# Shift and scale of a modulation: summed on VectorE along rows instead of collected on TensorE in one-column products

## The reference

```python
def adaln_pre_norm(x, c, g, w_mod, b_mod):
    mod = jax.nn.silu(c) @ w_mod + b_mod
    shift, scale, gate = jnp.split(mod, 3, axis=-1)
    h = rms_norm_2(x, g, NORM_EPS) * (1.0 + scale[:, None, :]) + shift[:, None, :]
    return h, gate
...
for i in range(DEPTH):
    h, gate = adaln_pre_norm(x, c, norm_g[i], w_mod[i], b_mod[i])
    ...
    x = x + gate[:, None, :] * y
```

## Time and profile before

| what | value |
|---|---|
| runs, median of 3 | 1061.03 us |
| the profiled execution's own time, given by its span from first to last instruction | 1066.7 us |
| TensorE busy | 1048.1 us (98%) |
| VectorE busy | 771.7 us (72%) |
| ScalarE busy | 590.3 us (55%) |
| POOL busy | 120.4 us (11%) |
| chain that ended last | TensorE 88%, VectorE 6% |

### The profile page before, as it was taken

One profiled execution on the slowest core, in us unless ns is written; L12 is line 12 of the kernel. 1 busy time (PEld: TensorE's weight loads), 2 busy tenths in 40 slices (PEclk: granted clock), 3 DMA queues, 4 the chain that ended last, 5 costly groups with the idle time before them and its releaser, 6 DMA issues.

```text
span 1066.7 us, 25458 instructions
## 1 busy us (share of the span) xinstructions
PE 1048.1 (98%) x10480; PEld 996.2 (93%) x10485; DVE 771.7 (72%) x1090; ACT 590.3 (55%) x900; POOL 120.4 (11%) x131
## 2 busy tenths in 40 slices
PE   9999999999999999999999999999999999999997
PEld 8966999999999899997899999999998999999985
DVE  5987666766789689768766676786676877775586
ACT  6586555555456783334555454564544667666452
POOL 0230010100000028841000000000000000000000
PEclk9999999999999999999999999999999999999999
DMA  8734687888634510002678777737653656556401
GB/s 308 251 90 137 216 286 266 271 296 280 204 122 155 163 61 5 3 11 74 217 250 287 255 252 264 276 121 228 197 192 112 212 181 199 171 195 196 143 2 59
DMA packets 83073, 192.23 MB, mean 180 GB/s; under 512 B 6000, under 2 KB 6912, under 8 KB 82992
## 3 DMA queue, kind: packets, MB, share of 16 engines
q1 hardware_dynamic: 74256, 159.93, 45.3%
q0 software_dynamic: 7584, 27.53, 7.8%
q10 hardware_dynamic: 1152, 3.59, 1.0%
HBM read 189.45 MB, written 1.05 MB: 179 GB/s over the span
## 4 chain that ended last, share of the span: by engine, by line
PE 88%; DVE 6%; issue 2%; ACT 2%; DMA 2%; POOL 0%; DVEq 0%; POOLq 0%; ACTq 0%
PE bank L2308 13%; PE bank L2310 13%; PE bank L2309 13%; PE bank L2659 5%; PE bank L2658 5%; PE bank L2660 5%; PE bank L2325 4%; PE bank L2345 4%; PE bank L2877 4%; PE bank L2275 2%; PE bank L2276 2%; PE bank L2277 2%; PE bank L2263 1%; PE bank L2265 1%; PE bank L2264 1%
## 5 line engine op out<-in xcount | busy, mean ns | idle before, releaser
L1350 DVE TENSOR_TENSOR w_lo<-raw,w_hi 128x1024 fp32r<-128x1024 f32 x295 | 357.8, 1223 | 199.2 <-ACT w_hi L737 198.7
L737 ACT ACTIVATE w_hi<-raw 128x1024 fp32r<-128x1024 f32 x295 | 310.3, 1059 | 291.4 <-PE bank L2310 150.4
L2308 PE MATMUL bank<-act_hi,w_hi 128*128 128x256 f32 x1200 | 334.0, 278 | 0.4 <-DVE w_lo L1350 0.3
L2309 PE MATMUL bank<-act_lo,w_hi 128*128 128x256 f32 x1200 | 332.9, 277 | 0.0
L2310 PE MATMUL bank<-act_hi,w_lo 128*128 128x256 f32 x1200 | 332.8, 277 | 0.0
L2308 PEld LDWEIGHTS bank<-act_hi,w_hi 128*128 128x128 f32 x1200 | 225.3, 188 | 1.7 <-DVE w_lo L1350 0.9
L2310 PEld LDWEIGHTS bank<-act_hi,w_lo 128*128 128x128 f32 x1200 | 225.3, 188 | 0.0
L2309 PEld LDWEIGHTS bank<-act_lo,w_hi 128*128 128x128 f32 x1200 | 225.0, 187 | 0.0
L2658 PE MATMUL bank<-w_hi,ff_hi 128*128 128x256 f32 x512 | 141.5, 276 | 0.0
L2659 PE MATMUL bank<-w_lo,ff_hi 128*128 128x256 f32 x512 | 141.5, 276 | 0.0
L2660 PE MATMUL bank<-w_hi,ff_lo 128*128 128x256 f32 x512 | 141.5, 276 | 0.0
(11 more groups left out here) (375 smaller groups left out, 1675.4 us busy)
## 6 DMA issues: line engine op xcount, KB each, us to landing
raw<-in_mlp_w_up_dram SPq DMA_DIRECT2D x64, 512.0 KB, 3.7
raw<-in_mlp_w_down_dram SPq DMA_DIRECT2D x64, 512.0 KB, 6.1
raw<-in_dil_w_in_dram SPq DMA_DIRECT2D x64, 512.0 KB, 4.1
mod_w<-in_w_mod_dram POOLq DMA_DIRECT2D x48, 512.0 KB, 5.9
raw<-in_conv_w_in_dram SPq DMA_DIRECT2D x32, 512.0 KB, 4.5
raw<-in_rwkv_w_rkv_dram SPq DMA_DIRECT2D x24, 512.0 KB, 4.1
raw<-in_dsa_w_in_dram SPq DMA_DIRECT2D x12, 512.0 KB, 8.1
raw<-in_dsa_w_o_dram SPq DMA_DIRECT2D x8, 512.0 KB, 4.5
```

Of the source, the lines that this page charges most:

```text
L737: act.activation(w_hi[:, slot, :], raw[:, slot, :], ACT.Copy).then_inc(hi_ready, 1)
L1350: dve.tensor_tensor(w_lo[:, slot, :], raw[:, slot, :], w_hi[:, slot, :].bitcast(F32), ALU.subtract).then_inc(lo_ready, 1)
L2308: pe.matmul(dst, w_hi[:, slot, at], hi[:, kt, :], start=begin, stop=False, skip_group_check=True)
L2309: pe.matmul(dst, w_hi[:, slot, at], lo[:, kt, :], start=False, stop=False, skip_group_check=True)
```

## The change

For shift and scale, the host lays `w_mod` out transposed: step k of part n brings output features 128k to 128k+127 as partitions, with the 1024 inputs along the row. silu(c) is needed as a row on all partitions: POOL loads `c_2` broadcast into `cond_row` ahead of each layer's weights, and ScalarE applies Silu to it in the MLP's first step, between the rounding of granule 7 and the relu. `weigh_mod` for shift and scale is then one VectorE instruction per step, a product of the two tiles with the sum along the row written as one column of `mod_col`. It writes the product back over `mod_w`. The gate part stays as it was. `mod_columns` goes, with both TensorE waits for its results; VectorE's addition of the bias reads `mod_col` in SBUF instead of PSUM. The number of weight bytes is the same.

```diff
         def mlp_plan(t):
-                        mod_all=t("mod_all", [P, 3 * D]),
+                        cond_row=t("cond_row", [P, D]), mod_unused=t("mod_unused", [P, D]), mod_gate=t("mod_gate", [P, D]),
...
             def modulation(l, between=()):
-                w = A["w_mod_2"][l].rearrange("(k p) (n c) -> n k p c", p=P, c=D)
+                w = A["w_mod_2"][l]
...
+                if l:
+                    for n in range(2):
+                        pool.wait_ge(mod_used[n], done)
+                pool.dma_start(M["cond_row"][:, :], A["c_2"][0].partition_broadcast(P)).then_inc(mod_loaded[0], 16)
...
-                def step(it, first_bank):
+                def step(it, first_bank, layer=None):
                     if isinstance(it, int):
                         split_block(base, 4, it)
+                        act.wait_ge(mod_loaded[0], 16 * (KT * layer + 2 + layer))
+                        act.activation(M["cond_row"][:, :], M["cond_row"][:, :], ACT.Silu).then_inc(cond_ready, 1)
                         relu(it, first_bank)
...
             def weigh_mod(l, n, k):
-                part, total = M["mod_w"][:, n, :], M["mod_all"][:, n * D:(n + 1) * D]
...
+                part = M["mod_w"][:, n, :]
+                rows = 16 * (KT * l + 1) + (16 * (l + 1) if n == 0 else 0)
+                dve.wait_ge(mod_loaded[n], k * 16 + rows)
+                if n < 2:
+                    if isinstance(k, int) and k == 0:
+                        dve.wait_ge(cond_ready, l + 2)
+                    to = mod_col[:, l, KT * n + k:KT * n + k + 1] if isinstance(k, int) else mod_col[:, l, bass.ds(k + KT * n, 1)]
+                    dve.scalar_tensor_tensor(part, part, 1.0, M["cond_row"][:, :], ALU.mult, ALU.mult,
+                                             accum_out=to).then_inc(mod_used[n], 1)
+                    return
+                total = M["mod_gate"][:, :]
...
             def modulation(l):
-                dve.wait_ge(mod_full, 4 * l + 2)
-                dve.tensor_tensor(mod_col[:, l, :], bank[(1, 3)[l]][:, 0:2 * KT], B_MOD[l], ALU.add).then_inc(mod_ready, 1)
+                for n in range(2):
+                    dve.wait_ge(mod_used[n], KT * (l + 1))
+                dve.tensor_tensor(mod_col[:, l, :], mod_col[:, l, :], B_MOD[l], ALU.add).then_inc(mod_ready, 1)
...
-            def mod_columns(l, part):
-                if part == 0:
-                    for n in range(2 if l else 3):
-                        pe.wait_ge(mod_used[n], KT * (l + 1))
...
-                for k in range(KT * part, KT * (part + 1)):
-                    mm = pe.matmul(bank[(1, 3)[l]][:, k:k + 1], M["mod_all"][:, k * P:(k + 1) * P], ones[:, 0:1], start=True, stop=True)
-                mm.then_inc(mod_full, 1)
...
             def rwkv_in():
-                turn_scaled(1, X, RKV_TURN, lambda: mod_columns(0, 0))
-                mod_columns(0, 1)
+                turn_scaled(1, X, RKV_TURN)
+                pe.wait_ge(mod_used[2], KT)
+                pe.wait_ge(up_relu, 2 * FF_STEPS)
                 mod_gate(0, (4, 5))
                 mod_gate(1, (4, 5))
...
-                    if n == 0:
-                        pe.wait_ge(mod_ready, 1)
...
                 fill(2, 1)
-                mod_columns(1, 0)
                 turn_scaled(2, xn, LATE_TURN)
-                mod_columns(1, 1)
...
-                            if n == 1 and half == q == 0:
-                                pe.wait_ge(mod_ready, 5)
```

More of the change, by code:

```diff
@@ L989, in step @@
                         split_hi(base, 8 + q, it)
-                step(0, 6)
+                step(0, 6, l)
                 with act.Fori(1, FF_STEPS - 1) as it:
@@ L1654, in weigh_mod @@
             def weigh_mod(l, n, k):
-                part, total = M["mod_w"][:, n, :], M["mod_all"][:, n * D:(n + 1) * D]
-                if isinstance(k, int):
-                    dve.wait_ge(mod_loaded[n], 16 * (KT * l + k + 1))
-                else:
-                    dve.wait_ge(mod_loaded[n], k * 16 + 16 * (KT * l + 1))
+                part = M["mod_w"][:, n, :]
[9 more added lines that the diff above has]
+                total = M["mod_gate"][:, :]
                 if isinstance(k, int) and k == 0:
@@ L1759, in gate_rows @@
                 for n, b in enumerate(banks):
-                    dve.wait_ge(mod_full, 4 * l + 3 + n)
+                    dve.wait_ge(mod_full, 2 * l + 1 + n)
                     to = gate[:, l, n * BLOCK:(n + 1) * BLOCK]
@@ L2712, in fill @@
                     pe.matmul(bank[b][:, 0:SEQ], ones, const[:, 0:SEQ], start=True, stop=True)
-            def mod_columns(l, part):
-                if part == 0:
-                    for n in range(2 if l else 3):
-                        pe.wait_ge(mod_used[n], KT * (l + 1))
-                    if l:
-                        pe.wait_ge(x_updated, 15)
-                    else:
-                        pe.wait_ge(up_relu, 2 * FF_STEPS)
-                for k in range(KT * part, KT * (part + 1)):
-                    mm = pe.matmul(bank[(1, 3)[l]][:, k:k + 1], M["mod_all"][:, k * P:(k + 1) * P], ones[:, 0:1], start=True, stop=True)
-                mm.then_inc(mod_full, 1)
             def mod_gate(n, banks=(5, 3)):
-                at = 2 * D + n * BLOCK
-                pe.matmul(bank[banks[n]][:, :], ones, M["mod_all"][:, at:at + BLOCK], start=True, stop=True).then_inc(mod_full, 1)
+                at = n * BLOCK
+                pe.matmul(bank[banks[n]][:, :], ones, M["mod_gate"][:, at:at + BLOCK], start=True, stop=True).then_inc(mod_full, 1)
             def rwkv_in():
                 base = STREAM["rkv"]
-                turn_scaled(1, X, RKV_TURN, lambda: mod_columns(0, 0))
-                mod_columns(0, 1)
+                turn_scaled(1, X, RKV_TURN)
+                pe.wait_ge(mod_used[2], KT)
+                pe.wait_ge(up_relu, 2 * FF_STEPS)
                 mod_gate(0, (4, 5))
@@ L3218, in laid_out @@
     arrays["w_iq"] = np.ascontiguousarray(iq.transpose(1, 0, 2, 4, 3, 5)).reshape(P, KT, IQ_COLS)
+    turned = arrays["w_mod_2"][:, :, :2 * D].reshape(2, D, 2, KT, P).transpose(0, 2, 3, 4, 1)
+    plain = arrays["w_mod_2"][:, :, 2 * D:].reshape(2, 1, KT, P, D)
+    arrays["w_mod_2"] = np.ascontiguousarray(np.concatenate([turned, plain], 1))
     arrays["const"] = np.concatenate([v.reshape(P, -1) for v in parts.values()], 1)
```

## The result

The changed kernel takes 1069.57 us (median of 15 runs, 1064.47 to 1072.71), the kernel before in the same comparison 1061.72 us (15 runs, 1060.56 to 1068.31). The ratio is 1.0065, 95% interval [1.0049, 1.008]: slower, by 7.85 us between the medians, outside the forecast's range.

A forecast was written before the change was run, and what follows sets the result against it. TensorE was taken as the bound (busy 1048.1 of 1066.7 us), in close races with VectorE at both entries. Terms -1.04 - 0.31, with 0 for VectorE's sums and ScalarE, gave -1.35: from median 1061.03 to 1059.7 us, range 1057.3 to 1063.7.

The forecast's parts named there:

- Entry of rkv, -1.04: Start of rkv: without the one-column products the second tile's turn and xx come 1.04 us earlier, then TensorE waits for the diagonal.
- Entry of conv, -0.31: Start of conv: of two bunches, 3.36 us, only 0.31 us is gained at the second block, VectorE being late next.
- VectorE's sums, 0: Weighings in the MLPs: 32 of 48 become summing products, 0.15 us more each, hidden by idle time; term 0.
- d: Extra time per VectorE summing instruction over the plain form's 1278 ns; taken as 0.15 us, at most 1.44.
- the upper bound: VectorE's summing form costed like the scan: four times 680 ns is 2720, 1.44 us more than the plain 1278 ns.
- the third rival: MLP ends: summing form slow, additions to X late; 1064.5 us at the upper bound, near 1063.5 at half rate; chance 0.12.
- ScalarE, 0: First step of each MLP: table load and pass, 2.34 us ahead of the relu, fit within 4.57 us of cover; term 0.
- the fourth rival: TensorE's waits at the entries lower its clock to 1.2 GHz, entry granules take twice as long; near 1070 us; chance 0.05.
- Behind both entries TensorE sets the pace again, and the gain stays: After the starts of rkv and conv: the gains of 1.04 and 0.31 us last, with nothing lost later.
- The stretches concerned do not depend on it, so I take the same difference from the median: Whole kernel: the median lies 5.7 us below the profiled span; the same -1.35 us is applied to it, giving 1059.7.
- the first two terms: The gains at the entries of rkv and conv, -1.04 and -0.31 us.

## Why the prediction was wrong

The two profiles, followed through the same marks, start times in us:

| mark | before | after | gain (-) or loss between marks |
|---|---|---|---|
| diagonal at rkv's entry | 295.90 | 295.01 | -0.89, first stage, differs between executions |
| first w_lo of rkv | 300.39 | 298.63 | -0.87, where the forecast had -1.04 |
| first w_lo at conv's entry | 703.12 | 701.15 | -0.21: +0.14 in the scan, -0.35 behind it, neither forecast |
| conv, block 2 | 718.12 | 715.81 | -0.34, the forecast's -0.31 |
| dil, first product | 822.92 | 823.71 | +3.10, nearly all of it the slow pitch in conv |
| end of the span | 1066.7 | 1066.2 | -1.29, late dil fast again in after (-1.6) |
| outside the span | +1.7 | +2.4 | +0.7 |

Point by point:

- *Entry of rkv, -1.04*: the mechanism was right, and the size near: 0.87. The second turn did start 1.03 earlier net of the lead, but `xx` only 0.88. That it is the columns is shown: with them put back this lead is 0. The 1.08 measured by conv's entry come nearer to 1.04 by luck, through the 0.35 behind the scan.
- *Entry of conv, -0.31*: right, 0.34. VectorE was late next, as said.
- *VectorE's sums, 0*: right. d is -0.05 us from start to start, not the 0.15 taken nor the 1.44 of the upper bound; the third rival falls. The case that the Trainium skill's "Vector Engine (DVE) Microarchitecture Reference" ("Points that are easy to get wrong") led one to expect, half rate, is not seen: 1217 ns with the sum, 1278 without.
- *ScalarE, 0*: right, with the relu 2.4 later and the down product unmoved.
- *The clock, the fourth rival*: it falls. The granted clock is 1.00 in every row above, at conv's entry too. Yet its premise, that taking products away lets TensorE wait and that waits cost something afterwards, was the right place to look, with another mechanism and another price.
- *"Behind both entries TensorE sets the pace again, and the gain stays"*: this step failed. The wait ahead of conv's block 2 was foreseen, and was costed at its length. Behind it TensorE drew the slow pitch for the whole stage: +3.10 between two marks, where 0 was forecast. That a wait can do this without anything else of the change is shown by one profile: put into the kernel before, it gave a slow conv, where the five profiles of that kernel's conv without it are fast. The other direction isn't shown. The order that takes the wait out of the kernel after gave one fast conv and three slow ones (two of the three with columns ahead of conv), and two further profiles of the kernel after's conv are slow ahead of the wait. So the loss in conv goes with the missing products, through the wait at block 2 in the profile compared here and through conv's entry in others; the odds of each are not known.
- *"The stretches concerned do not depend on it, so I take the same difference from the median"*: this failed too, and cost more. The 5.7 us between the profile's span and the median were dil's slow pitch, and the profiled execution's own time was not the span but some 1.7 more. By its times the kernel before has a fast dil in most executions, the kernel after in 1 of 15 at most; why the change shifts these odds is open. A median moves by such odds, and no sum over one profile shows it. From dil's first product to the end of the span the second profile of the kernel before takes 1059.7 - 822.61 = 237.1 us, the kernel after 1066.2 - 823.71 = 242.5: +5.4.
- *Outside the span*: the time is 1.7 us above the span in executions of the kernel before and of all kernels made from it, 2.4 us in all made from the kernel after. This +0.7 us was not thought of, and nothing here tells what it is.

Added up against the kernel before with both stages at 113.3 ns: -1.08 - 0.34 + 3.10 + 5.4 + 0.7 = 7.8 us. Between the two executions compared the difference is 1068.6 - 1061.4 = 7.2, which is this sum less the 0.6 by which the first stage happened to be shorter in the second. That the medians differ by 7.85, nearly the sum, is in part luck: the profiled execution of the kernel after lies 1.0 below its median. The forecast had only the first two terms, and the first of them in part.

Open: what decides which pitch is drawn. conv's level does not carry over to dil (fast conv and slow dil with the order changed, and in the profile before; for the reverse there is only a time of 1065.6 with the added wait). Putting the columns back at rkv and conv brought the fast group back in four of ten executions, though nothing at dil's entry was changed. A wait isn't needed for a change of pitch. The late part of dil in the kernel after went from slow to fast at 960.2, where another kind of product begins (weights and activations change places) and nothing waits. Shortly ahead of that a few products of this kind are set in. In the first profile of the kernel before the pitch goes from slow to fast there, at 958.1, for some 12 matmuls and back; in the second, at 952.6, from fast to slow for 13 and back; in the kernel after it stays. A property of the moment of the restart or of the change of kind would fit all this; it was not shown.

## What to carry to other kernels

A wait in front of a long unbroken stream of matmuls is not worth its length alone: look at what the stream does behind it, by counting matmuls per stretch in both profiles, even where the engine shows as fully busy at the full clock. Useless work that happens to stand ahead of such a stream can be worth more than it costs. Neither cure tried was reliable: filling the wait with other products never helped, and bringing the producer's work forward took the wait away in all four kernels that had it, while conv was fast in one profile of four. One profile shows one draw, so look at the single times and at more than one profile. When the span of the profile lies 0.5% off the median, find out which stage makes the difference before the sum is carried over.

## What the runs showed of the hardware

- A stream of weight loads and 128x256 fp32r matmuls runs at 113.3 or 117.8 ns from start to start, both at a granted clock of 1.00; it kept one level for 767 intervals in conv and 671 behind the wait. In these profiles the level changed where TensorE started again behind a wait (715.81 in the kernel after) or where another kind of product began (960.2 in the kernel after). Which one it is differs between executions of one kernel.
- With four 256-column fp32 filler products ahead of dil in the kernel before, all seven executions had times of the slow level, and with eight one-column products all ten.
- A product with a sum along the row takes 1217 ns for 1024 fp32 elements and 80 ns for the read-out, against 1278 ns for multiply and add; from start to start 1.15 us against 1.20.
